# The last four experts of a mixture-of-experts layer, multiplied together or one by one

## The reference

```
def hierarchical_moe(h, ...):
    ...                                  # combine: two weights per token
    for gi in range(N_GROUPS):           # 4 groups of 8 experts
        hid = silu(t @ w_gate[gi]) * (t @ w_up[gi])      # per expert, 1024 -> 256
        hid = hid * combine[:, gi, :, None]
        y = y + einsum("tef,efd->td", hid, w_down[gi])   # 256 -> 1024
h = layer_norm(DEEPNORM_ALPHA * h + ffn, ln2_g, ln2_b)
...
qkv = rms_norm(h) @ w_qkv                # second block, attention
```

## Time and profile before

| | |
|---|---|
| median of 3 runs | 1005.76 us (1004.15 to 1006.05) |
| profiled execution, first to last instruction | 1007.2 us |
| PE busy in it | 947.1 us |
| DVE, ACT busy | 572.0, 389.0 us |
| HBM read | 224.50 MB |

### The profile page before, as it was taken

One profiled execution on the slowest core, in us unless ns is written; L12 is line 12 of the kernel. 1 busy time (PEld: TensorE's weight loads), 2 busy tenths in 40 slices (PEclk: granted clock), 3 DMA queues, 4 the chain that ended last, 5 costly groups with the idle time before them and its releaser, 6 DMA issues.

```text
span 1007.2 us, 14412 instructions
## 1 busy us (share of the span) xinstructions
PE 947.1 (94%) x5957; PEld 736.1 (73%) x5957; DVE 572.0 (57%) x906; ACT 389.0 (39%) x525; POOL 32.3 (3%) x49
## 2 busy tenths in 40 slices
PE   8999989999999999496989999999999999999997
PEld 7999886677775534142558888888888888888885
DVE  5885473996664102000087657666566786666564
ACT  4554502774252111010056455443343453433341
POOL 1410100003000000000000000000000000000000
PEclk9999999999999999898999999999999999999999
DMA  9824330455789999999896622555454444554421
GB/s 326 251 106 167 113 142 1 143 192 192 309 334 362 420 419 420 419 420 420 347 364 225 222 87 89 177 215 189 167 199 176 167 168 168 195 216 174 167 83 42
DMA packets 67564, 226.39 MB, mean 225 GB/s; under 512 B 4129, under 2 KB 5441, under 8 KB 55857
## 3 DMA queue, kind: packets, MB, share of 16 engines
q1 hardware_dynamic: 65648, 220.24, 58.0%
q0 software_dynamic: 1632, 5.26, 1.6%
q10 hardware_dynamic: 224, 0.07, 0.0%
HBM read 224.50 MB, written 1.05 MB: 224 GB/s over the span
## 4 chain that ended last, share of the span: by engine, by line
PE 78%; DMA 9%; DVE 8%; ACT 2%; issue 2%; SPq 1%; DVEq 0%; ACTq 0%
PE bank L1495 16%; PE bank L1484 11%; PE bank L1485 6%; PE bank L1201 5%; PE bank L747 5%; DMA arena<-in_expert_w_up 4%; PE bank L1349 4%; DMA ring<-in_expert_w_up 3%; PE bank L1069 2%; PE bank L764 2%; PE bank L1111 2%; PE bank L1411 2%; PE bank L1353 2%; PE bank L796 1%; PE bank L1339 1%
## 5 line engine op out<-in xcount | busy, mean ns | idle before, releaser
L2585 DVE TENSOR_TENSOR w_lo<-ring,w_hi 128x2048 fp32r<-128x2048 f32 x76 | 170.5, 2285 | 75.8 <-ACT w_hi L1836 75.7
L1836 ACT ACTIVATE w_hi<-ring 128x2048 fp32r<-128x2048 f32 x76 | 141.3, 1915 | 94.0 <-PE bank L1495 86.3
L1484 PE MATMUL bank<-xT_lo_hi,w_hi 128*128 128x512 f32 x480 | 170.0, 398 | 0.0
L1485 PE MATMUL bank<-xT_lo_hi,w_lo 128*128 128x256 f32 x480 | 134.8, 281 | 0.0
L1484 PEld LDWEIGHTS bank<-xT_lo_hi,w_hi 128*128 128x128 f32 x480 | 90.2, 188 | 22.2
L1495 PE MATMUL bank<-w_hi,hidden_hi 128*128 128x512 f32 x256 | 100.0, 391 | 0.0
L1495 PE MATMUL bank<-w_hi,hidden_lo 128*128 128x512 f32 x256 | 99.8, 390 | 0.0
L1495 PE MATMUL bank<-w_lo,hidden_hi 128*128 128x512 f32 x256 | 99.7, 389 | 0.0
L1485 PEld LDWEIGHTS bank<-xT_lo_hi,w_lo 128*128 128x128 f32 x480 | 90.7, 189 | 0.5
L1201 PE MATMUL bank<-ring,arena 128*32 128x512 f32 x256 | 54.1, 642 | 21.8 <-DMA arena<-in_expert_w_up 21.8
L1934 ACT ACTIVATE arena<-bank 128x256 f32<-128x256 f32 x64 | 21.1, 382 | 109.9 <-PE bank L1485 106.1
(11 more groups left out here) (584 smaller groups left out, 1737.3 us busy)
## 6 DMA issues: line engine op xcount, KB each, us to landing
ring<-in_mlp_w_up SPq DMA_DIRECT2D x32, 1024.0 KB, 6.9
ring<-in_mlp_w_down SPq DMA_DIRECT2D x32, 1024.0 KB, 6.1
ring<-in_w_in SPq DMA_DIRECT2D x22, 1024.0 KB, 8.0
ring<-in_expert_w_gate SPq DMA_DIRECT2D x15, 1024.0 KB, 12.3
ring<-in_expert_w_up SPq DMA_DIRECT2D x15, 1024.0 KB, 15.6
ring<-in_expert_w_down SPq DMA_DIRECT2D x14, 1024.0 KB, 19.9
arena<-in_expert_w_down SPq DMA_DIRECT2D x12, 1024.0 KB, 21.8
ring<-in_attn_w_qkv SPq DMA_DIRECT2D x12, 1024.0 KB, 11.0
```

The lines of the kernel that those rows point to most:

```text
L1484: mm(cube(B[4 + c], 2), w_hi[:, at], both_parts(k), start=(k == 0), stop=False)
L1485: last = mm(B[4 + c][:, 0:SEQ], w_lo[:, at], xTH[:, k, 0:SEQ], start=False, stop=(k == KD - 1))
L1836: act(whi[:, n % 2, half], slot(u)[:, half], ACT.Copy).then_inc(S("split_hi"), 1)
L2585: tt(wlo[:, u % SLOTS, half], slot(u)[:, half], f32(whi[:, n % 2, half]), ALU.subtract).then_inc(S("split_lo"), 1)
```

## The change

Items 1 to 3 concern the last quad and the loads behind it, item 4 the start.

1. On PE `up_last` takes the place of `up_quad` for the last quad. It goes expert by expert, waiting for one unit at a time. One expert's eight slices are dealt over the four strips (two slices each), into bank 5 or 7, so that the bank holds four partial sums. DVE (experts 0 and 2) or ACT (1 and 3) copies the bank to the new tile `strips`, and one matmul with a constant 128 x 32 matrix `fold` adds the four partial sums and puts them in the expert's strip of bank 4. Fillers stand ahead of the first expert (6), between an expert's matmuls and its fold (3), and behind the fold (8, not after the last).
2. The last `down_quad` signals after its first half, ACT copies that half while the second is multiplied, and `scatter_last` scatters one half and then the other. DVE's statistics follow the order of the banks, 0, 2, 1, 3. ACT loads the square root's table after the copy of `hTs` instead of ahead of it.
3. Units 15, 16 and 17 wait for the same counts of `moe_unit` as before, which are now reached one by one; unit 15 goes to the other half of `w_hi`, the one that doesn't lie over unit 47.
4. The first constants are 201 columns wide, since `fold` is among them, and the warm-up matmuls read all of them. Some semaphores are merged: PE waits for four small early loads where it waited for one.

```
+        def up_last():
+            q = QUADS - 1
+            j = moe_unit(None, q)
+            for e in range(4):
+                moe_landed(None, j + e)
+                w_ = moe_slot(None, j + e).rearrange("p b (k n) -> p b k n", k=KD)
+                for kk in range(2):
+                    for g in range(4):
+                        k = 2 * g + kk
+                        last = mm(cube(B[5 + 2 * (e % 2)][CAP * g:CAP * (g + 1), :], 2), xs[:, k, P + CAP * e:P + CAP * (e + 1)], w_[:, :, k, :], start=(kk == 0), stop=(kk == 1))
+                last.then_inc(S("moe_unit"), 1)
+                keep_going(3, 6, P // 2)
+                pe.wait_ge(S(("strip_dve", "strip_act")[e % 2]), e // 2 + 1)
+                mm(B[4][CAP * e:CAP * (e + 1), :], C("fold"), strips[:, e % 2, :], start=True, stop=True).then_inc(S("folded"), 1)
+                if e < 3:
+                    keep_going(8, 6, P // 2)
...
+        def scatter_last():
+            q = QUADS - 1
+            for half in range(2):
+                pe.wait_ge(S(("y_act", "y_dve")[half]), nth(None, q))
+                for i in range(NT):
+                    mm(B[2 * i + half], hTs[:, (2 + i) * P:(3 + i) * P], ysb[:, half * 512:(half + 1) * 512], start=False, stop=True).then_inc(S("scat"), 1)
...
                 if last_one:
                     scatter(s_, order[n - 1], False, False)
-                    keep_going(30, 5, P // 2)
-                if q < SPILLED:
+                    keep_going(6, 6, P // 2)
+                if last_one and s_ is None:
+                    up_last()
+                elif q < SPILLED:
                     up_quad(s_, q)
...
+            final = s_ is None and q == QUADS - 1                 # ACT, quad()
+            if final:
+                for e in (1, 3):
+                    sc.wait_ge(S("moe_unit"), moe_unit(None, q) + e + 1)
...
+                    act(strips[:, 1, :], B[7], ACT.Copy).then_inc(S("strip_act"), 1)
+                sc.wait_ge(S("folded"), 4)
...
-            if q == QUADS - 1:
-                warm_sqrt()
...
             act(hTs, B[4], ACT.Copy).then_inc(S("hT_out"), 1)
-            sc.wait_ge(S("moe_unit"), down_count(s_, q))
+            if q == QUADS - 1:
+                warm_sqrt()
+            sc.wait_ge(S("moe_unit"), down_count(s_, q) - (1 if final else 0))
...
-            hi_halves(U_TWO + u, u)
+            hi_halves(U_TWO + u, u + 1)
...
-SMALL = {..., "zero": 1}
+SMALL = {..., "zero": 1, "fold": CAP}
```

More of the change, by code:

```diff
@@ L65 @@
 HALVES = ["eye2"] + [f"level{i}" for i in range(LEVELS - 1)]
-SMALL = {"hmask": DN_H, "idx4": NG, "desc4": NG, "desc8": NE, "freq": HALF, "eps5": 1, "eps5a": 1, "eps6": 1, "one": 1, "zero": 1}
+SMALL = {"hmask": DN_H, "idx4": NG, "desc4": NG, "desc8": NE, "freq": HALF, "eps5": 1, "eps5a": 1, "eps6": 1, "one": 1, "zero": 1, "fold": CAP}
 def const_layout():
@@ L85, in shape_constants @@
         "neg": np.where(q <= r, 0.0, NEG), "iota": q + 0 * r,
-        "rep": (q % 32 == r) & (r < META), "before": (q % NE < q // NE) & (r >= 0),
+        "rep": (q % 32 == r) & (r < META), "fold": r % CAP == np.arange(CAP)[None, :], "before": (q % NE < q // NE) & (r >= 0),
         "hmask": (r // 32 == np.arange(DN_H)[None, :]) & (r % 32 < META),
@@ L257, in build @@
     xs_spill = cube(reg(KD * SPILL), KD)
+    strips = cube(xs_spill.rearrange("p k c -> p (k c)"), 2)
     ysb = X1[:, 2, :]
@@ L1239, in down_quad @@
                         last = mm(B[6 + half][at, :], hTs[:, k * P + CAP * e:k * P + CAP * (e + 1)], w_[e][:, k * D + half * 512:k * D + (half + 1) * 512], start=(k == 0), stop=(k == 1))
-            last.then_inc(S("moe_unit"), 1 if s_ is None and q == SPILL_QUAD else 2)
+                if half == 0 and s_ is None and q == QUADS - 1:
+                    last.then_inc(S("moe_unit"), 1)
+            last.then_inc(S("moe_unit"), 1 if s_ is None and q in (SPILL_QUAD, QUADS - 1) else 2)
         def down_spill():
@@ L1311, in experts @@
                     down_quad(s_, q)
-            scatter(s_, order[-1], False, True)
+            if s_ is None:
+                scatter_last()
+            else:
+                scatter(s_, order[-1], False, True)
             return flag
@@ L1328, in attention @@
             for u in range(6):
-                w_hi, w_lo = whi[:, u % 2, :], wlo[:, (U_TWO + u) % SLOTS, :]
+                w_hi, w_lo = whi[:, (u + 1) % 2, :], wlo[:, (U_TWO + u) % SLOTS, :]
                 pe.wait_ge(S("split_hi"), SPLIT_HI + 2 * u + 2)
@@ L1608, in _ @@
         first_split(2)
-        sc.wait_ge(S("raw_pad"), 1)
+        sc.wait_ge(S("stacked"), 1)
         for c in range(N_DN):
@@ L1622, in _ @@
         sc.wait_ge(S("ba_out"), 3)
-        act(be, ba[:, :, 0:DN_H], ACT.Exp, scale=-1.0).then_inc(S("be_exp"), 1)
+        act(be, ba[:, :, 0:DN_H], ACT.Exp, scale=-1.0).then_inc(S("ga_ln"), 1)
         sc.wait_ge(S("ga_abs"), 1)
@@ L2070, in _ @@
         first_low(4)
-        dve.wait_ge(S("be_exp"), 1)
+        dve.wait_ge(S("ga_ln"), 1)
         line(ts(be, be, 1.0, None, ALU.add))
         line(nc.vector.reciprocal(be, be))
-        dve.wait_ge(S("ga_ln"), 2)
+        dve.wait_ge(S("ga_ln"), 3)
         line(stt(gu, gu, 0.0, gt, ALU.max, ALU.add))
@@ L2135, in _ @@
         dve.wait_ge(S("proj_out"), 25)
[L2136 removed]
+        dve.wait_ge(S("dn_small_in"), 64)
         for i in range(NT):
@@ L2139, in _ @@
         line(last)
-        dve.wait_ge(S("stacked"), 2)
+        dve.wait_ge(S("stacked"), 3)
         for lv in range(INNER):
@@ L2473, in quad @@
         def quad(s_, q):
+            if s_ is None and q == QUADS - 1:
+                for e in (0, 2):
+                    dve.wait_ge(S("moe_unit"), moe_unit(None, q) + e + 1)
+                    if e == 2:
+                        dve.wait_ge(S("folded"), 1)
+                    nc.vector.tensor_copy(strips[:, 0, :], B[5]).then_inc(S("strip_dve"), 1)
             dve.wait_ge(S("sg_made"), nth(s_, q))
@@ L2493, in part_of, with statistics @@
             return x[:, n // 2, (n % 2) * 512:(n % 2 + 1) * 512]
-        def statistics(count):
-            for n in range(4):
-                dve.wait_ge(S("scat"), count + n + 1)
+        def statistics(count, order):
+            for at, n in enumerate(order):
+                dve.wait_ge(S("scat"), count + at + 1)
                 nc.vector.bn_stats(stats[:, 1 + n // 2, n % 2, :], B[n]).then_inc(S("moe_out"), 1)
@@ L2548, in _ @@
                 collect(s_)
-            statistics(4 * PASSES)
+            statistics(4 * PASSES, range(4))
             dve.wait_ge(S("moe_out"), 4 * PASSES + 8)
```

26 lines of the change are left out of this document (14 added, 12 removed).

## The result

| | changed kernel | kernel before, beside it |
|---|---|---|
| median | 1014.65 us (1013.3 to 1015.0, 4 runs) | 1004.95 us (1003.88 to 1006.05, 4 runs) |
| ratio | 1.0086, 95% interval 1.0070 to 1.0102 | |
| profiled execution, span | 1012.8 us | 1007.2 us |
| profiled execution, device time | 1015.0 us | not listed |

The change costs 9.7 us by the medians; the ratio with its interval gives 8.6 (7.0 to 10.2). Slower was forecast, but as +3.6 us and 1009.4, and the range ended at 1011.5. About half of the loss is in nothing that was priced.

What follows compares the result with a forecast made beforehand. PE's own fillers, folds and switches, not a load's landing, were to set the experts' end. Terms +5.4 - 1.0 - 1.1 + 0.3 = +3.6 us took the median 1005.76 to 1009.4; range 1006.0 to 1011.5.

Steps and rivals of the forecast that it cites:

- So what is won or lost here should reach the end whole.: Behind the experts: after the square root only PE and DVE work without loads follows, so gains or losses stay.
- The median of the runs shown lies at 1005.76, so 1009.4.: Basis of the total: profiled span 1007.2 would become 1010.8, and the median 1005.76 would become 1009.4.
- the start's 0.3: Warm-up at the start: 32 more columns in 24 records cost +0.24 to +0.38, taken as +0.3 us.
- the +5.4: From the last quad's fillers to the down matmuls: down starts at 506.2 instead of 500.83, +5.4 us.
- 5.81 us with DVE, 5.72 with ACT.: One expert of `up_last`: strips, fillers, copy, fold and switches take this period, by which engine copies.
- Rival 1: Last quad: switches between strips and full width are free, sum +2.4 us, 1008.2; chance 0.20.
- PE never waits for a landing: Last quad: each expert starts after its unit landed; PE is 10.7 us behind at the last expert.
- the term -1.0: Down and scatter: copying and scattering by halves takes 3.55 instead of 4.55 us, -1.0 us.
- the term -1.1: Square root behind the experts: earlier unit 15 ends the 1.1 us wait in ACT's queue, -1.1 us.
- Rival 2: Last quad: landings set the end, faster, -2.9 us, 1002.9; decided if down starts before 502.6; chance 0.13.
- Rival 3: Last quad: the clock falls in the new sequence, one spell at 0.50 costing 1.8 us, 1011.2; chance 0.11.
- Rival 4: Last quad: strips of one expert do not run side by side, +20.6 us on top, 1030; chance 0.02.

Runs made afterwards that it cites:

- e1: The kernel before, unchanged, profiled once more: 1005.56 us, span 1003.4.
- e6: Changed kernel with 30 fillers instead of 6 in the branch that is never taken: 1010.5 us, ratio 1.0049.
- e2: Kernel before with 8 fillers fewer in the branch that is never taken: 1009.01 us, ratio 1.0034.
- e3: Changed kernel with 8 fillers more in the branch that is never taken: 1012.15 us, ratio 1.0063.
- e5: Changed kernel with 10 instead of 6 fillers in the branch that is never taken: 1016.52 us, ratio 1.0111.
- e11: Changed kernel with no fillers instead of 6 in the branch that is never taken: 1011.11 us, ratio 1.0059.
- e7: Kernel before with item 2 alone and the other half of `w_hi` for units 15 to 20: 1006.01 us, ratio 1.0006.
- e4: e3 without the eight fillers behind each of the first three folds, code place kept by fillers in the never-taken branch: 1005.66 us, ratio 0.9999.
- e9: e8 with 16 more fillers in the branch that is never taken: 1004.24 us, ratio 0.9988.
- e10: Changed kernel with PE's four wide fillers moved from ahead of the overflow branch to behind it: 1016.08 us, ratio 1.0095.
- e8: e4 with warm-up matmuls of 169 columns as before, fold matrix still loaded with the first constants: 1005.13 us, ratio 0.9994.

## Why the prediction was wrong

**"So what is won or lost here should reach the end whole."** This step failed, and with it the largest part. It took the work behind the experts as fixed. The place of that code in the instruction stream is part of the change: +5.45 us of the 9.4 between e1 and the changed execution (3.74 of pause, the rest at half clock), and 4.2 of the 9.7 between the medians (e6). e2, e3, e5, e6 and e11 show it, since they move that code and touch nothing that runs. One sign of it was there in advance: two q8 packets behind the branch in the kernel before as well, at 509.0 and 515.0. That a boundary stood 6 records away only the moves show, and a list of waits shows neither while they are hidden.

**"The median of the runs shown lies at 1005.76, so 1009.4."** The basis was wrong. The span was compared with device times, from which it lacks 2.2 us, so an execution that was 3.6 us long was taken for one that was 1.4 long. Its extra time lay just where the change works: 33.25 us from the fillers to the transposes, 30.26 in e1. The working gave 33.25 + 5.4 - 1.0 - 1.1 = 36.55 us for the changed kernel, and 35.66 came. Against e1 it would have been +6.3, with the start's 0.3 +6.6. The term that the wrong basis mis-sized is the +5.4: from the first fillers to the down matmuls the changed kernel takes 24.21 us (25.0 by the working), e1 17.20 and not 19.63, so it is +7.0. Without the pause the time would have been within the range: e6 has 1010.5.

**"5.81 us with DVE, 5.72 with ACT."** Right mechanism, size 0.15 too large: 5.65 and 5.57. The strips followed six fillers after 1.37 us, which is 6 x 0.227 and 0.01 more; behind eight fillers it was 1.93, 0.11 more. The 0.19 taken from full-width 512-column matmuls is not the price there: the 4 switches give back 0.4 us. Rival 1 (the switch is free) was right on the first of them and not on the others. The rest is the fold, which starts 0.08 to 0.09 us earlier than in the working (2.74 us behind the strips with DVE, 2.66 with ACT).

**"PE never waits for a landing", its own sequence sets the end.** Right. No landing stands in the chain, unit 15's high parts are followed by an idle ACT until the square root's input is there (511.44), down to scatter is 3.57 us (3.55 forecast), scatter to square root 4.79 (4.92 by the earlier trace rows). The difference is a reading: the square root follows the aggregate of the statistics, which was ready at 510.10, and not the row at 510.13. So the term -1.0 held in the changed kernel, and the term -1.1 was -1.3. ACT's branch lies in the 0.65 us of issue ahead of the high parts and cost nothing, since ACT was idle for 1.41 us behind them. e7 adds what was not said: the first term is worth nothing without the second.

**The start.** +0.3 us forecast for the wider warm-up. The second warm-up takes 4.25 us instead of 3.61, and the transposes stand at 13.99 in the timeline, against 13.80 and 13.89. Over all executions they stand at 13.99 to 14.42 with the wide one and at 12.89 to 14.05 with the narrow one, so the size is right, and hardly above the chance of one execution.

**The rivals.** Rival 2 (the landings set the end) is what e4 and e9 made true by taking the fillers out; its -2.9 us was too much (e9: -1.2 by the ratio), since its sum took the same wrong basis. Rival 3's half clock came, but behind the pause and not in the last quad, where the clock stayed at 1.00 from 480 to 510. Rival 4 did not occur.

## What to carry to other kernels

An edit ahead of a taken branch, even in code that is never run, moves the code behind it; look at the engine's instruction packets there and count what stands between the branch target and the next wait for instructions, and try one or two paddings before judging a change. Fillers that cover a wait become the bound as soon as the wait is gone; here 24 of them cost 5.2 us (e3 to e4), and what the finer waits bring without them is at best 1.2 (e9). Make the sum against an execution whose device time is the median's, and compare spans with spans.

## What the runs showed of the hardware

- Behind PE's taken branch two instruction packets come 5.8 to 6.2 us apart, and PE goes on 2.4 to 2.8 us behind the one it needs: 3.5 us from the end of the scatter for the branch target (e10), and a pause of up to 4.53 us for the block behind it (e5).
- The fetch for a taken branch starts while matmuls ahead of it still run: with fillers of 3.6 us ahead of the branch the first packet came 0.8 to 1.1 us behind the scatter's end (changed, e3, e5, e11), without them 0.8 (e10).
- A matmul on one strip ran beside the next expert's three other strips (e4: 483.31 and 483.32), but its own strip was then two records behind, and the set took 2.69 us with it, where an expert's strips alone take 1.86. A full-width filler behind a fold started 0.98 us after it, when its two records were through (changed kernel: 482.98 and 483.96).
- The clock fell to 1.2 GHz behind waits of PE of 1.50 us (e8, and the kernel before ahead of its up matmuls), 1.83 (e2), 2.36 (e7), 3.50 (e10), 3.74 (changed) and 4.53 (e5), and held at 2.4 GHz behind 1.43 (e1) and 0.63 (e11). The execution of the kernel before held it behind 1.97, ahead of its transposes, so the length of the wait alone doesn't say it; the runs don't settle what does.
